# Gate tiles of the index stage ahead of its waits, and those of the sample steps at other steps

## What is computed

```python
qkv_sb, qkv_fox, f_logit, qkv_dsa, q_idx, k_idx, w_idx, gate_logit = jnp.split(h @ w_in, offs, axis=-1)
...
isc = jnp.einsum('bqhd,bkd->bqhk', qib, k_idx).astype(jnp.float32) * (IDX_DIM ** -0.5)
isc = jnp.einsum('bqhk,bqh->bqk', jax.nn.relu(isc), wib.astype(jnp.float32)) * (IDX_HEADS ** -0.5)
...
vals, idx = lax.top_k(isc, topk)
...
gates = jax.nn.sigmoid(gate_logit.reshape(b, t, N_BRANCH, D_MODEL))
merged = jnp.sum(gates * y, axis=2)
return merged @ w_out, new
```

## Time and profile before

| | us |
|---|---|
| median of 3 runs (2592.31 to 2592.51) | 2592.48 |
| the profiled execution, its own time | 2593.86 |
| its span, first to last instruction | 2592.0 |
| TensorE busy | 2457.0 |
| VectorE busy | 1187.8 |
| ScalarE busy | 565.3 |

### The profile page before, as it was taken

One profiled execution on the slowest core, in us unless ns is written; L12 is line 12 of the kernel. 1 busy time (PEld: TensorE's weight loads), 2 busy tenths in 40 slices (PEclk: granted clock), 3 DMA queues, 4 the chain that ended last, 5 costly groups with the idle time before them and its releaser, 6 DMA issues.

```text
span 2592.0 us, 40797 instructions
## 1 busy us (share of the span) xinstructions
PE 2457.0 (95%) x16820; PEld 2049.7 (79%) x16820; DVE 1187.8 (46%) x2626; ACT 565.3 (22%) x1250; POOL 62.9 (2%) x100
## 2 busy tenths in 40 slices
PE   7999999999998899999999999999999899999998
PEld 6999997655656579999989999865556565899997
DVE  3455522203667435556326664221056764256642
ACT  3000013113544312000122001220235332310011
POOL 0000000000012100000000000000000120000000
PEclk8999999999999899999999999999999998999999
DMA  8465532541269534556651333324323693413332
GB/s 302 163 228 209 174 114 70 148 146 62 87 212 290 189 116 142 208 209 215 214 195 63 107 122 105 123 71 140 106 86 135 208 305 126 161 66 110 111 110 70
DMA packets 299561, 389.91 MB, mean 150 GB/s; under 512 B 33678, under 2 KB 245386, under 8 KB 299379
## 3 DMA queue, kind: packets, MB, share of 16 engines
q1 hardware_dynamic: 281538, 339.52, 39.2%
q0 software_dynamic: 10752, 38.93, 4.8%
q10 hardware_dynamic: 7088, 8.87, 0.9%
HBM read 377.66 MB, written 9.62 MB: 149 GB/s over the span
## 4 chain that ended last, share of the span: by engine, by line
PE 85%; DMA 6%; DVE 4%; ACT 2%; SPq 1%; issue 1%; ACTq 0%; DVEq 0%
PE PS L683 24%; PE PS L730 12%; PE PS L841 12%; PE PS L895 9%; PE PS L1088 4%; DMA QR<-w_ada 3%; PE PS L610 3%; PE PS L666 3%; PE PS L650 2%; PE PS L795 2%; PE PS L786 2%; PE PS L1110 2%; PE PS L1102 2%; PE PS L1047 2%; PE PS L1017 1%; PE PS L1057 1%
## 5 line engine op out<-in xcount | busy, mean ns | idle before, releaser
L841 PE MATMUL PS<-RING,H 128*128 128x384 f32 (+1 forms) x960 | 307.2, 482 | 0.0
L841 PEld LDWEIGHTS PS<-RING,H 128*128 128x128 f32 x960 | 181.8, 190 | 121.0 <-issue 0.6
L895 PE MATMUL PS<-H,RING 128*128 128x384 f32 x672 | 231.5, 500 | 8.4 <-ACT QR L1389 8.4
L683 PE MATMUL PS<-OT,RING 128*128 128x192 f32 x1216 | 222.5, 326 | 0.0
L683 PE MATMUL PS<-H,RING 128*128 128x192 f32 x1216 | 215.5, 331 | 0.0
L683 PE MATMUL PS<-OT,QR 128*128 128x192 f32 x1216 | 210.0, 326 | 0.0
L683 PEld LDWEIGHTS PS<-H,RING 128*128 128x128 f32 x1216 | 200.6, 192 | 5.9 <-issue 5.7
L895 PEld LDWEIGHTS PS<-H,RING 128*128 128x128 f32 x672 | 128.2, 195 | 95.5 <-issue 9.8
L683 PEld LDWEIGHTS PS<-OT,RING 128*128 128x128 f32 x1216 | 201.8, 190 | 0.0
L683 PEld LDWEIGHTS PS<-OT,QR 128*128 128x128 f32 x1216 | 199.7, 190 | 0.0
L1216 ACT ACTIVATE QR<-QR 128x384 f32<-128x384 f32 x76 | 39.7, 523 | 509.2 <-DVE QR L1697 509.2
(11 more groups left out here) (269 smaller groups left out, 3597.6 us busy)
## 6 DMA issues: line engine op xcount, KB each, us to landing
RING<-ffn_w_in SPq DMA_DIRECT2D x80, 1024.0 KB, 7.2
QR<-w_ada SPq DMA_DIRECT2D x66, 1024.0 KB, 9.0
RING<-w_in SPq DMA_DIRECT2D x64, 768.0 KB, 6.0
RING<-ffn_w_out SPq DMA_DIRECT2D x32, 768.0 KB, 4.7
RING<-ffn_w_out SPq DMA_DIRECT2D x32, 640.0 KB, 5.6
QKT<-cache_sb_k SPq DMA_DIRECT2D x16, 768.0 KB, 5.8
QR<-cache_sb_v POOLq DMA_DIRECT2D x16, 768.0 KB, 5.0
QKT<-cache_fox_k SPq DMA_DIRECT2D x16, 768.0 KB, 6.0
```

Source lines behind the costliest of these rows:

```text
L683: mm = pe.matmul(PS[:, bank, GROUP[g]], a[:, k, :], x[:, k, :], start=(k == 0), stop=(k == 3))
L841: mm = pe.matmul(PS[:, n % 3, 0:width], H[:, k, tt * P:(tt + 1) * P], w[:, k, :], start=(k == 0), stop=(k == KD - 1))
L895: mm = pe.matmul(PS[:, bank, 0:T], w[:, k, (n % 3) * P:(n % 3 + 1) * P], H[:, k, :], start=(k == 0), stop=(k == KD - 1))
```

## The change

In the index stage tile 6 and tile 7 each wait only for the first relu (which frees banks 0 and 1); the wait for the relu of two heads back now stands behind the tile, ahead of the scores that need it. ScalarE takes tile 6 after the relu of sample head 0 (n = 2) and no longer after that of head 1; tile 7 as before after that of head 2 (n = 4). In the sample steps tile 21 goes from step 5 to step 4, tile 22 from step 12 to step 6, and tile 23 from step 19 to step 15, on TensorE and ScalarE alike, since both read the same table. SP's order is the same.

```diff
-GATE_STEP = dict(zip((0, 1, 2, 3, 5, 12, 19), range(17, 24)))
+GATE_STEP = dict(zip((0, 1, 2, 3, 4, 6, 15), range(17, 24)))
...
                     if h >= 2:
+                        pe.wait_ge(relu_ready, l * 6 + 1)
+                        gate_tile(GATE_SCORE[h - 2], h - 2, 0)
                         pe.wait_ge(relu_ready, l * 6 + (h + 1))
-                        gate_tile(GATE_SCORE[h - 2], h - 2, 0)
...
-                        if n in (3, 4):
-                            take_gate(GATE_SCORE[n - 3], n - 3)
+                        if n in (2, 4):
+                            take_gate(GATE_SCORE[n // 2 - 1], n // 2 - 1)
```

## The result

The changed kernel takes 2557.41 us (median of 4 runs, 2556.02 to 2559.04) against 2592.49 for the kernel before beside it (4 runs, 2592.31 to 2596.3): a ratio of 0.9861, 95% interval 0.9844 to 0.9879. The kernel before spread from 2576.6 to 2597.6 in the later series, so single runs differ by up to 21 us, and where a few us decide I go by the stretches in the traces.

A forecast was written before the change was run, and what follows sets the result against it. TensorE, holding 85% of the chain, was taken as the bound. Per layer 6.6 + 5.35 + 3.0 = 14.95 us, twice 29.9, takes the profiled 2593.86 to 2564.0; less 1.38 for the median gives 2562.6, range 2556 to 2570.

The forecast's parts named there:

- (1): Index stage: tile 6 starts right after the first scores, head 2's scores come earlier; 6.6 us gained per layer.
- (2): Sample steps 4 to 7: tiles 21 and 22 at steps 4 and 6 take 28.7 us against 34.07; 5.35 gained per layer.
- (3): Steps 8 to 23: tile 22 leaves step 12, tile 23 goes from 19 to 15; 3.0 us gained per layer.
- the 68 to 69 that were named: Sign for the third term in the profile after: steps 8 to 19 in about 68 to 69 us.
- the 4.9 less 2.0: Steps 8 to 23: a net removed tile saves 4.85 us, minus three transfer waits of 0.67 it had hidden; 2.9 left.
- The cross-check by the free share of the DMA engines: Steps 8 to 19: DMA engines stood free only 5% or 3% of the time, 3.6 and 2.1 us, mean 2.9.
- A: Steps 8 to 23: transfers take the third term whole, bias rows queuing behind key and value loads; 2568.6 us, chance 0.16.
- B: Index stage: the clock falls anyway, so 4.2 us instead of 6.6 per layer; 2567.4 us, chance 0.08.
- C: Tile-free steps 12 to 14 and 16 to 22: TensorE stays at 1.2 GHz; slower by 34, 2626.6 us, chance 0.03.
- D: Steps 8 to 23: waits at L2045 only move, tile 22 won whole, third term 5.3; 2558.0 us, chance 0.07.
- E: Index stage: head-2 wait really guards bank 0, or ScalarE delays head 1's relu; first term lost, 2575.8 us, chance 0.03.
- The estimate by the figure of the Trainium skill: Steps 8 to 19: at 358 GB/s the bytes need 61 us, transfers would not bind, third term 4.85; not adopted.

The follow-up runs named there:

- a_t21: Kernel before with only tile 21 moved, from step 5 to step 4: 2578.79 us, ratio 0.9957.
- a_index: Changed kernel with the old tile table (tiles 21, 22, 23 at steps 5, 12, 19), so the index part alone: 2579.04 us, ratio 0.9958.
- b_t23: Kernel before with only tile 23 moved, from step 19 to step 15: 2587.36 us, ratio 0.9987.
- light kernels: Half the cached value rows unloaded in FOX and DSA: kernel before 2575.79 us; changed kernel with tile 23 at step 19, 2546.90; changed kernel, 2545.32.
- b_at19: Changed kernel with tile 23 back at step 19 instead of 15: 2560.84 us, ratio 0.9896.
- b_at22: Changed kernel with tile 23 at step 22 instead of 15: 2558.96 us, ratio 0.9885.
- b_after_again: The changed kernel run again unaltered (the repetition), beside the kernel before: 2558.54 us, ratio 0.9884.

## Why the prediction was right

The forecast was 2562.6 us, 29.9 less; measured were 35.1 less, and 31.4 in the repetition (30.0 by its ratio). Both are inside 2556 to 2570, on the low side. The prediction's "21 gate tiles per layer" are 24; nothing rests on that number.

**(1) Index stage, 6.6 a layer.** The size holds (6.7), as do the mechanism (the wait belonged to the scores), the clock of 1.00 and VectorE's last sum, 5.7 us sooner where 5.8 was worked out. One step failed: that tile 7's wait is only for what has long happened, "so it costs and gains nothing". In the kernel before it was; once tile 6 is early it is not, and tile 7's edit gives 1.1 of the 6.7. The working checked head 2's scores against the relu that they need at their new time, and left out the same check for head 1's relu.

**(2) Steps 4 to 7, 5.35 a layer.** 5.36 and 5.37, with no low clock and no wait at the output transpose; the weights of tile 21 were no trouble (a_t21: 4.8 for that tile alone). In other kernels with the same tiles in these steps the same stretch takes less (31.2 us in a_index) or more (35.1 in b_t23), so 5.4 is that profile's value, 2.5 to 6.4 what the traces have.

**(3) Tiles 22 and 23, 3.0 a layer.** This is the mis-sized term. Steps 8 to the end fell by 6.5 and 3.9 us in the profiles of before and after, and by 3.9 on the means of many stretches (100.3 to 96.45, known to about 1.3). On these means steps 8 to 19 fell by 4.5, to 66.85 us, below the 68 to 69 that were named, and the steps behind them grew by 0.6, from 29.0 to 29.6, which fits waits that only moved. Its make-up was wrong twice. I had tile 23's move from 19 to 15 cancel out, one step gaining what the other lost: it is worth 2.3, and most of that goes when the loads are halved. Why steps 19 to 22 need a cover less, perhaps because the last keys are on their way by then, is argued and not shown; with the tile at step 22 the end was 97.2, between the two. And I gave tile 22 the 4.9 less 2.0: it was worth 1.6. The 2.0 were all put down to transfers; in the light kernels 2.3 of 5.1 went as well, 0.9 to VectorE's late output row, 1.0 to steps 16 to 18, and 0.5 to where the clock fell. One error was too high and the other too low, so that their sum came near is in part luck. The cross-check by the free share of the DMA engines (3.6 and 2.1 us) gave the right order, but it isn't a bound: steps 8 to 19 fell by 4.8 and 5.0, since the window moved up to 0.9 MB less afterwards, and a share can be above 1 (1.01 in the earlier trace rows).

The rivals: A (transfers keep the length) fell with those 4.9 us. B (clock falls anyway in the index stage) fell with the 1.00. C (the clock falls in tile-free steps and stays down) fell for the changed kernel: steps 8 to 19 ran at 1.00 in both layers, in the repetition too. Its first half is real, as b_at19 and b_at22 show, but after two steps the clock was back. D (tile 22 won whole) fell with its 1.6, though its 2558.0 us are the nearest of all the times to both medians: they came about in another way. E fell with tile 6 starting directly behind the scores. The estimate by the figure of the Trainium skill ("DMA: Bandwidth & Descriptors", section Bandwidth), 358 GB/s and with it 4.85 for term (3), is near the fall in steps 8 to 19 but above the 3.9 of the whole term. That section gives the 358 as a core's part when both cores of its memory stream, and this kernel runs on one core; the changed kernel's trace passes it, with 383 GB/s over 30 us of loads near its start:

```profile
20.00:50.00 30.00, 22.90 (x327) 18.61 (x327) 10.92 (x46) 12.34 (x30) 0.00 (x0) 0.82 1.06 383
```

In steps 8 to 19 the share was 0.98 to 0.99 already at 315 GB/s, so 358 is neither the limit nor free room there; what rate a busy share of 1 stands for differs between these two stretches.

## What to carry to other kernels

A piece of independent work belongs ahead of the wait that the next dependent piece needs, with only the wait for its own buffer before it; then check each later wait against the new times, not the old. Filler work pays most where the engine would wait anyway: beside another engine's long step, or in a stretch that waits for transfers. A filler that is taken away uncovers everything that ran beside it, not only the transfers. Judge such moves of 1 to 3 us by stretches of many traces, since the median of a kernel here moves by more.

## What the runs showed of the hardware

The granted clock makes the same instructions take different times in different executions: steps 4 and 5 with the same tiles took 17.45 us (a_index) and 19.12 (before), and the kernel before spread over 0.8% in the later series. The wait of 2.98 us at the output transpose came again to the hundredth wherever it stands, and the clock behind it did not (1.00 or 0.88 or 0.78 in step 5). The changed kernel's eight runs lie between 2554.5 and 2562.0 us; they are too few to show that it is steadier.

In steps 22 and 23, where the 128x128 transposes of the keys have ended and only small matmuls are left, TensorE was at 1.2 GHz for a part in all 28 layer stretches of the fourteen profiles, with a tile at step 22 too (2.50 us for a group of values that takes 1.42), and it was at that level when the branch stage began, though it was busy for most of the time (16.25 of the 23.70 us from 868.6 to 892.3 in the kernel before, at a mean of 0.57). In one layer each of a_index, b_after_again, b_at19 and b_t23 it had been back at 2.4 GHz for some us in between. After a fall in the middle steps, which have those transposes, the clock was back within two steps and stayed up. Whether the transposes are the reason is not shown: no run takes them out.
